# Strassen's seven products for the first 512 rows of paired weight panels

## The chip, the cores and the metric

One NeuronCore of a Trainium2 chip runs the whole program. The metric is the device time of one execution in microseconds (us). Engines are named as the profile names them: PE (TensorE) with PEld (its weight loads), DVE (VectorE), ACT (ScalarE), POOL (GpSimd), SP (SyncE, which issues most of the transfers). "L774" is line 774 of the kernel before.

## The reference, cut to what matters

Two transformer blocks run one after the other on 256 tokens of width 2048, in float32. Nearly all of the arithmetic is in products of the activations (256 x K) with large weights:

```python
proj = rmsnorm(x, g) @ w_in          # 2048 x 6144: differential attention and retention
x = x + mixed @ w_o                  # 2048 x 2048
xq = hx @ w_xq; xk = hm @ w_xk; xv = hm @ w_xv; x = x + xo @ w_xo
x = x + (silu(hf @ w_gate) * (hf @ w_up)) @ w_down      # 2048 x 5632 twice, 5632 x 2048
...
mod = silu(c) @ w_ada + b_ada        # one row times 2048 x 6144
proj = h @ w_in_2; g = sigmoid(h @ w_merge + b_merge)
merged = g_a * (y_a @ w_br_attn) + g_p * (y_p @ w_br_pool)
out = x + gate * rmsnorm(merged @ w_out)
```

## The kernel before, in words

**Panels.** `panel_table` (L152) cuts every weight into panels of 512 columns. A panel has two PSUM banks, one for each tile of 128 tokens, and sums over its rows in chunks of 512 rows. Even and odd panels use different pairs of banks (`bank_of`, L293), so one pair is emptied while the other is filled. The order is: 12 panels of `w_in` (kinds tq, v, rg), 4 each of `w_o` (o), `w_xk`, `w_xv`, `w_xq`, `w_xo`, then gate and up panels in turn (g, u), interrupted after four and eight of each by four panels of `w_down` (d, d, and e at the end), then one kv panel, 8 panels of `w_in_2` (q, ga, pu, gp), 8 of `w_merge` (m), 4 each of the two branches (ba, bp) and 4 of `w_out` (out). A panel of four chunks has 8 halves.

**Halves.** A chunk of 512 x 512 weights is one item of 1 MB, loaded by SP into one of 4 buffers (`raw`, RAWS = 4). It is used in two halves of 256 rows (128 x 1024 elements). For each half ACT rounds to `whi` (L1194) and DVE makes the rest `wlo = raw - whi` (L1762); both have 4 slots (HALVES = 4). The activations are held the same way as high and low parts, in the buffers `a` and `b`. PE then runs, for each 128 rows and each token tile, three matmuls with the activations as the stationary 128x128 operand and 512 weight columns moving (L774 to L776): high by high, high by low, low by high. A half is 2 x 2 x 3 = 12 matmuls, and there are 720 halves.

**What sets the order.** Every engine runs a program written out in full, one list of steps, one for each half. At its step n each of ACT and DVE makes the half three ahead, then one piece of a queued job (`Jobs`: attention, retention, turning of results into new stationary operands), then, at the end of a panel, takes the sum out of PSUM (`begin`). Nothing is reordered at run time: what waits holds up all that stands behind it on its engine. The waits that matter are these four. ACT makes half n only after PE has finished half n-4 (`e.wait_ge(s["half"], n - HALVES + 1)`). DVE makes the low part after ACT's high part. PE waits for the low part. SP loads item i into the buffer of item i-4 only when the low part of the last half of that item is made (`wait_taken`, L1928).

**The ada items.** `w_ada` is one row times a matrix and is done on DVE, one multiply-add over 128x2048 for each item of 1 MB (`add_ada`, L1449, L1460). 32 of these items are put between the weight items from the first up panel on, one for every two items, and 16 from the second merge panel on in the same rhythm. They use the same four buffers and the same SP queue.

Of the kernel before, what the change touches and what calls it, by code (L numbers as in the profile page):

```python
# [9 lines left out]
F32 = mybir.dt.float32  # L10
# [5 lines left out]
D = 2048  # L16
S = 256
# [51 lines left out]
def layouts(v):  # L69
# [8 lines left out]
Step = namedtuple("Step", "p half n tiles made end")  # L78
# [16 lines left out]
    "b_merge", "b_gate0", "b_gate1", "gain0", "gain1", "out",  # L95
# [5 lines left out]
    "x_hi", "x_lo", "mem_hi", "mem_lo", "st_hi",  # L101
# [50 lines left out]
def panel_table(a):  # L152
# [3 lines left out]
    def rows(version, n, first=0):  # L156
        return tuple((j * PW, (version, first + j)) for j in range(n))

    w_in, w_o, w2 = a["w_in"][0], a["w_o"][0], a["w_in_2"][0]
# [3 lines left out]
        ("tq", 4, 3072), ("tq", 5, 3584), ("v", 2, 4096), ("rg", 0, 5120), ("v", 3, 4608), ("rg", 1, 5632))]  # L163
    for kind, w, met in (("o", w_o, rows("mix", 4)), ("xk", a["w_xk"][0], mem), ("xv", a["w_xv"][0], mem),
                         ("xq", a["w_xq"][0], rows("hx", 4)), ("xo", a["w_xo"][0], rows("xo", 4))):
        table += [Panel(kind, j, w, j * PW, met, None) for j in range(4)]
    for first, n, down in ((0, 4, "d"), (4, 4, "d"), (8, 3, "e")):
        for i in range(first, first + n):
            table.append(Panel("g", i, a["w_gate"][0], i * PW, rows("hf", 4), None))
            table.append(Panel("u", i, a["w_up"][0], i * PW, rows("hf", 4), None))  # L170
        h = tuple((i * PW, ("h", i)) for i in range(first, first + n))
        done = first if down == "d" else 0
        table += [Panel(down, done + j, a["w_down"][0], j * PW, h, "last" if (down, j) == ("e", 3) else None)
                  for j in range(4)]
    table += [Panel("kv", 0, w2, 1024, mod, "first")]
    table += [Panel(kind, i, w2, col, mod, None) for kind, i, col in (
        ("q", 0, 0), ("ga", 0, 1536), ("q", 1, 512), ("ga", 1, 2048), ("pu", 0, 2560), ("gp", 0, 3584),
        ("pu", 1, 3072), ("gp", 1, 4096))]
    table += [Panel("m", 2 * n + b, a["w_merge_2"][0], b * D + n * PW, mod, None) for n in range(4) for b in range(2)]
    for n in range(4):  # L180
        table.append(Panel("ba", n, a["w_branch_attn_2"][0], n * PW, rows("ya", 2), None))
        table.append(Panel("bp", n, a["w_branch_pool_2"][0], n * PW, rows("yp", 2), None))
    table += [Panel("out", j, a["w_out_2"][0], j * PW, rows("mg", 4), "last" if j == 3 else None) for j in range(4)]
    return table
# [9 lines left out]
class Stream:  # L194
# [3 lines left out]
    def __init__(self, panels):  # L198
        self.panels, self.index = panels, {(p.kind, p.i): i for i, p in enumerate(panels)}
        self.base, n = [], 0  # L200
        for p in panels:
            self.base.append(n)
            n += 2 * len(p.rows)
        self.total = n
        self.end = self.base[1:] + [n]
        self.steps = self._steps()
        kv = self.index["kv", 0]
        self.pool_halves = range(self.base[kv], self.end[kv])
        self.items, self.item_of, self.ada_before = [], [], {}
        self._items()  # L210
        last, before, lies = {}, {}, {}
        for i, p in enumerate(panels):
            for j, (_, key) in enumerate(p.rows):
                last[key] = self.base[i] + 2 * j + 2
                at = place_of(*key)
                if lies.get(at, key) != key:
                    before[key] = lies[at]
                lies[at] = key
        self.free = {key: last[before[key]] if key in before else 0 for key in last}

    def _steps(self):
        steps, done = [], 0
        for i, p in enumerate(self.panels):
            n = 2 * len(p.rows)
            a, b = {"first": (0, HALVES), "last": (n - HALVES, n), None: (n, n)}[p.stagger]
            order = ([(h, (0, 1)) for h in range(a)] + [(h, (t,)) for t in range(2) for h in range(a, b)]
                     + [(h, (0, 1)) for h in range(b, n)])
            for h, tiles in order:
                made = min(done + HALVES, self.total)
                done += 1 in tiles  # L230
                steps.append(Step(i, h, self.base[i] + h, tiles, made, h == n - 1))
        return steps

    def _items(self):
        early = [(g, k) for g in range(2) for k in range(16)]
        late = [(2, k) for k in range(16)]
        count, ada = 0, []
        for i, p in enumerate(self.panels):
            for kc in range(len(p.rows)):
                self.ada_before[len(self.item_of)] = ada  # L240
                self.item_of += [len(self.items)] * 2
                self.items.append(("w", i, kc))
                count, ada = count + 1, []
                for todo, first in ((early, self.index["g", 0] + 1), (late, self.index["m", 1])):
                    if todo and i >= first and count % 2 == 0:
# [1744 lines left out]
```

## Time and profile before

| | |
|---|---|
| runs of the kernel before | 2140.12 us median of 3 (2139.46 to 2142.23) |
| the profiled execution's own time | 2138.73 us |
| its span | 2136.8 us |
| PE, DVE, ACT, POOL busy | 2111.2, 1258.9, 964.7, 72.1 us |
| granted PE clock, mean | 0.998 |

The span is what the trace covers; 1.9 us of the execution lie around it. A matmul's end is modelled, so its row shows 0.39 us while the next one starts 0.227 us later; the distance of starts is its cost. A busy share says how much of the time an engine had work, not whether it was waited for.

### The profile page before, as it was taken

What the parts mean: (1) busy time and instruction counts of PE and PEld (TensorE: products, weight loads), DVE (VectorE), ACT (ScalarE), POOL (GpSimd) and SP (SyncE); (2) the same over time, 40 slices, a digit from 0 to 9 for tenths busy, and PEclk for the clock granted to TensorE, in tenths of its full rate; (3) what the DMA queues carried; (4) which work ended last, traced back from release to release, by engine and by line L of the source; (5) the groups of instructions that cost most, each with busy time, mean ns of one, the idle gap of its engine ahead of it and who ended that gap; (6) DMA issues with size and microseconds to landing.
All of it is one profiled execution on the core that took longest, in us unless ns stands there. A gap on an engine that the chain in (4) does not pass through costs nothing.

```text
span 2136.8 us, 23563 instructions
## 1 busy us (share of the span) xinstructions
PE 2111.2 (99%) x9574; PEld 1743.9 (82%) x9574; DVE 1258.9 (59%) x1334; ACT 964.7 (45%) x1236; POOL 72.1 (3%) x94
## 2 busy tenths in 40 slices
PE   8999999999999999999999999999899999999998
PEld 7888888888888888888888888888688888888786
DVE  5556555644444556777677554555655545777755
ACT  6545444644443444443344433445644544444343
POOL 1000000000000000000000000000310000000000
PEclk9999999999999999999999999999999999999999
DMA  9555557555544459787887555554465556888653
GB/s 337 160 185 180 162 182 249 198 187 187 197 138 158 151 188 336 277 289 268 291 293 256 197 185 191 196 190 166 146 226 160 176 182 209 290 313 287 206 186 118
DMA packets 206284, 453.62 MB, mean 212 GB/s; under 512 B 7888, under 2 KB 10080, under 8 KB 199904
## 3 DMA queue, kind: packets, MB, share of 16 engines
q1 hardware_dynamic: 200272, 432.04, 59.1%
q0 software_dynamic: 5616, 19.94, 3.1%
q8 instruction: 76, 1.25, 0.2%
q14 instruction: 32, 0.26, 0.0%
q10 hardware_dynamic: 288, 0.13, 0.0%
HBM read 447.88 MB, written 4.19 MB: 212 GB/s over the span
## 4 chain that ended last, share of the span: by engine, by line
PE 89%; issue 6%; DVE 2%; DMA 1%; ACT 1%; POOL 0%; SPq 0%; DVEq 0%; ACTq 0%; POOLq 0%
PE ps L774 28%; PE ps L776 28%; PE ps L775 27%; PE ps L416 2%; DMA raw<-in_w_in_dram 1%; PE ps L535 1%; PE ps L556 1%; DMA FR<-in_x_t_dram 1%; PE ps L637 0%; PE ps L621 0%; DVE wlo L1762 0%; PE ps L671 0%; PE ps L660 0%; ACT FR L1057 0%; DVE FR L1583 0%
## 5 line engine op out<-in xcount | busy, mean ns | idle before, releaser
L1762 DVE TENSOR_TENSOR wlo<-raw,whi 128x1024 fp32r<-128x1024 f32 x712 | 869.0, 1224 | 648.7 <-ACT whi L1194 645.2
L1194 ACT ACTIVATE whi<-raw 128x1024 fp32r<-128x1024 f32 x720 | 758.6, 1057 | 755.4 <-PE ps L776 744.7
L774 PE MATMUL ps<-whi,ah 128*128 128x512 f32 x1888 | 751.1, 398 | 4.8 <-DVE wlo L1762 2.2
L776 PE MATMUL ps<-whi,al 128*128 128x512 f32 x1888 | 736.6, 390 | 0.0
L775 PE MATMUL ps<-wlo,ah 128*128 128x512 f32 x1888 | 735.6, 390 | 0.0
L774 PEld LDWEIGHTS ps<-whi,ah 128*128 128x128 f32 x1888 | 354.9, 188 | 77.0 <-issue 4.5
L776 PEld LDWEIGHTS ps<-whi,al 128*128 128x128 f32 x1888 | 354.6, 188 | 75.7
L775 PEld LDWEIGHTS ps<-wlo,ah 128*128 128x128 f32 x1888 | 355.2, 188 | 71.2 <-issue 0.2
L774 PE MATMUL ps<-whi,bh 128*128 128x512 f32 x992 | 392.6, 396 | 0.7 <-DVE wlo L1762 0.7
L776 PE MATMUL ps<-whi,bl 128*128 128x512 f32 x992 | 386.7, 390 | 0.0
L775 PE MATMUL ps<-wlo,bh 128*128 128x512 f32 x992 | 386.3, 389 | 0.0
L776 PEld LDWEIGHTS ps<-whi,bl 128*128 128x128 f32 x992 | 186.2, 188 | 39.6
L774 PEld LDWEIGHTS ps<-whi,bh 128*128 128x128 f32 x992 | 186.3, 188 | 39.3 <-DVE wlo L1762 1.2
L775 PEld LDWEIGHTS ps<-wlo,bh 128*128 128x128 f32 x992 | 186.4, 188 | 38.4 <-issue 1.0
L1460 DVE SCALAR_TENSOR_TENSOR FR<-raw,Z,FR 128x2048 f32<-128x2048 f32 x45 | 105.6, 2346 | 0.0
L1794 POOL TENSOR_TENSOR Z<-Z 128x2 f32<-128x2 f32 (+1 forms) x18 | 11.7, 655 | 1523.7 <-DVE Z L1237 826.9
L813 ACT ACTIVATE bh<-ps 128x512 fp32r<-128x512 f32 x38 | 22.8, 599 | 80.1 <-PE ps L416 56.6
L1247 DVE TENSOR_TENSOR bl<-ps,bh 128x512 fp32r<-128x512 f32 x38 | 26.3, 691 | 47.4 <-ACT bh L813 47.4
L416 PEld LDWEIGHTS ps<-ident,FR 128*128 128x128 f32 x312 | 38.1, 139 | 13.8 <-issue 3.5
L416 PE MATMUL ps<-ident,FR 128*128 128x128 f32 x312 | 46.1, 272 | 3.2 <-DVE FR L1276 2.2
L804 ACT ACTIVATE junk<-X 128x512 bf16<-128x512 f32 x38 | 23.9, 629 | 37.7 <-DVE X L1298 30.9
L844 ACT ACTIVATE FR<-ps,Z 128x512 f32<-128x512 f32 x22 | 15.2, 689 | 29.9 <-PE ps L776 29.9
(192 smaller groups left out, 751.2 us busy)
## 6 DMA issues: line engine op xcount, KB each, us to landing
raw<-in_w_in_dram SPq DMA_DIRECT2D x83, 1024.0 KB, 5.2
raw<-in_w_ada_dram SPq DMA_DIRECT2D x48, 1024.0 KB, 4.8
raw<-in_w_gate_dram SPq DMA_DIRECT2D x44, 1024.0 KB, 5.2
raw<-in_w_up_dram SPq DMA_DIRECT2D x44, 1024.0 KB, 5.2
raw<-in_w_down_dram SPq DMA_DIRECT2D x44, 1024.0 KB, 5.1
raw<-in_w_merge_dram SPq DMA_DIRECT2D x32, 1024.0 KB, 5.7
raw<-in_w_o_dram SPq DMA_DIRECT2D x16, 1024.0 KB, 5.1
raw<-in_w_xk_dram SPq DMA_DIRECT2D x16, 1024.0 KB, 5.0
```

The source lines that it names most:

```text
L416: ins = e.transpose(T[b].ap[:, kk * 256 + t * 128:kk * 256 + t * 128 + 128], src[:, t, (2 * b + kk) * 128:(2 * b + kk + 1) * 128], ident[: ...
L535: ins = e.matmul(A[0].ap[:, t * S:(t + 1) * S], QTC[:, d, t * 128:(t + 1) * 128], XKT[:, 4 * h + d, :], start=(d == 0), stop=(d == 3))
L556: ins = e.matmul(A[b].ap[:, dd * S:(dd + 1) * S], XV[:, k, c0:c0 + 128], PTC[:, k, :], start=(k == 0), stop=(k == 1))
L774: e.matmul(o, h, wh, start=(st.half == 0 and kk == 0), stop=False)
L775: e.matmul(o, h, wl, start=False, stop=False)
L776: ins = e.matmul(o, lo, wh, start=False, stop=(st.end and kk == 1))
L804: squares[:] = name, done(e.activation(junk[:, 0:n], in_, ACT.Square, accum_out=acc), name)
L813: ins = e.activation(hi, bank.ap[:, :], ACT.Copy)
L1194: done(e.activation(whi[:, n % HALVES, :], raw[:, i % RAWS, h * 1024:(h + 1) * 1024], ACT.Copy), "hi")
L1247: ins = e.tensor_tensor(lo, bank.ap[:, :], hi.bitcast(F32), ALU.subtract)
L1460: done(e.scalar_tensor_tensor(acc, src, csilu[:, k:k + 1], acc, ALU.mult, ALU.add), "ada")
L1762: done(e.tensor_tensor(wlo[:, n % HALVES, :], src, whi[:, n % HALVES, :].bitcast(F32), ALU.subtract), "lo")
```

## The change

**Pairs.** 80 of the 95 panels are put together in 40 pairs (f, s): all but the first two of `w_in`, the last two of the e and of the out panels, kv, and the ba and bp panels. In each pair the first 512 rows of both panels are met by Strassen's algorithm in Winograd's form. The 2 x 2 blocks are: activations, two token tiles by two halves of 256 rows; weights, two halves of rows by the two panels. Seven products of 6 matmuls take the place of 8 blocks of 6 matmuls. All other rows stay as they were. A product has one weight half and one token tile, and it counts as one entry in the whi/wlo slots, just like an ordinary half.

**Sums of weights.** Four of the seven products use a sum of weight blocks. DVE makes each with one 128x1024 tensor_tensor in place in `raw` (`sum_weights`), which waits for DVE's own last low part. The sums are spread so that each stands before a different entry's low part. The sums of activations (`make_forms`) are made once for each of 11 first chunks.

**Sums of results.** M3, M1, M2 and others add up in PSUM. ACT copies a bank in the middle of the sum three times per pair into a buffer `side` (`snapshot`), DVE makes one of them a difference, and when a panel ends, DVE adds or subtracts the side buffer for three of the pair's four banks (`summed`); residual and merge panels have it added to their other term beforehand (`add_ahead`).

**Order.** A pair of four chunks runs (N is an ordinary half of the first panel): M3, M5, N, M1, M2, N, M6, N, N, M7, N, M4, N, then six halves of the second panel. The first panel of a pair takes the banks that the pair before left earliest. No job runs at M3, M5 and M1. The ada items are placed anew: two in each of the first ten gate/up pairs (after the third and fourth chunk of u), three in each of the four d pairs and in each of the four merge pairs, one in each of the first four branch panels.

```diff
+PRODUCTS = {"M3": (0, 0, True, 1, 0), "M5": (0, 1, True, 1, 1), "M1": (1, 1, False, 0, 0),
+            "M2": (1, 0, False, 1, 0), "M6": (1, 1, True, 0, 0), "M7": (1, 1, True, 0, 1), "M4": (1, 1, False, 1, 1)}
...
+    def _pair(self, f, s):
+        i_f, i_s = self._item(f, 0), self._item(s, 0)
+        b11, b21, b12, b22 = (i_s, 0), (i_s, 1), (i_f, 0), (i_f, 1)
...
+        product("M3", b22, start=True, job=False)
+        product("M5", b12, b11, start=True, job=False)
+        normal(f, *next(todo), snap=("s5", q))
+        product("M1", b11, start=True, job=False)
+        product("M2", b21, start=True, snap=("s1", q))
+        if chunks == 4:
+            normal(f, *next(todo))
+        product("M6", b22, b12)
+        normal(f, *next(todo), snap=("v", q))
+        if chunks == 4:
+            normal(f, *next(todo))
+        product("M7", b11, b22, minus=True)
+        normal(f, *next(todo), snap=("s3", q))
+        product("M4", b21, b22, aside=q)
+        for c, hf in todo:
+            normal(f, c, hf)
+        for c in range(1, chunks):
+            for hf in range(2):
+                normal(s, c, hf)
+            if self.panels[s].kind in ("u", "d") and c > (1 if self.panels[s].kind == "u" else 0):
+                self._load_ada(self._early, 1)
+            elif self.panels[s].kind == "m":
+                self._load_ada(self._late, 1)
...
+            def snapshot(what, q):
+                form, place = {"s5": ("M5", (0, 0)), "s1": ("M1", (1, 0)), "s3": ("M7", (0, 1))}[what]
...
+                e.wait_ge(s["half"], at[form] + 1)
...
+                done(e.activation(side_of(pair[place[0]], place[1]), bank_of(pair[panel], t)[:, :], ACT.Copy), "snap")
...
+            def summed(p, t, dst):
+                wait_sum(p, t)
+                wait_side(p, t)
+                took(add_side(p, t, dst, bank_of(p, t)[:, :]), p, t)
+            def difference(q):
+                (f, second), at = stream.pairs[q]
+                e.wait_ge(s["half"], at["M6"] + 1)
...
+                done(e.tensor_tensor(v, bank_of(second, 1)[:, :], v, ALU.subtract), "snap_v")
...
+            def sum_weights(n):
+                item, h, add, minus, nth = stream.entries[n]
+                for loaded in (item, add[0]):
+                    e.wait_ge(s[f"raw{loaded % RAWS}"], 16 * (loaded // RAWS + 1))
+                if count["lo"]:
+                    e.wait_ge(s["lo"], count["lo"])
...
+                done(e.tensor_tensor(place((item, h)), place(add), place((item, h)), ALU.subtract if minus else ALU.add),
+                     "t_sum")
+            for _, at in stream.pairs:
+                sums_before |= {at["M3"]: at["M5"], at["M5"] + 1: at["M6"], at["M2"]: at["M7"], at["M6"] + 1: at["M4"]}
...
             def wait_taken(i):
...
+                    if i in stream.last_sum_of:
+                        e.wait_ge(s["t_sum"], stream.last_sum_of[i])
+                    n = stream.last_of_item[i]
                     e.wait_ge(s["lo_pool" if n in stream.pool_halves else "lo"], stream.lo_count(n))
```

## Rows read from the trace of the kernel before

**Rows 1.** The page: busy time of the engines, and shares of the last chain.

```profile
PE 2111.2 (99%) x9574; PEld 1743.9 (82%) x9574; DVE 1258.9 (59%) x1334; ACT 964.7 (45%) x1236; POOL 72.1 (3%) x94
...
PE 89%; issue 6%; DVE 2%; DMA 1%; ACT 1%; POOL 0%; SPq 0%; DVEq 0%; ACTq 0%; POOLq 0%
```

**Rows 2.** Groups of instructions: busy us, mean ns, then idle time before.

```profile
L1762 DVE TENSOR_TENSOR wlo<-raw,whi 128x1024 fp32r<-128x1024 f32 x712 | 869.0, 1224 | 648.7 <-ACT whi L1194 645.2
...
L1460 DVE SCALAR_TENSOR_TENSOR FR<-raw,Z,FR 128x2048 f32<-128x2048 f32 x45 | 105.6, 2346 | 0.0
...
L1298 DVE TENSOR_TENSOR X<-ps,X 128x512 f32<-128x512 f32 x38 | 24.5, 686 | 6.3 <-PE ps L776 6.3
...
L828 ACT ACTIVATE FR<-ps 128x512 f32<-128x512 f32 x16 | 9.6, 599 | 25.4 <-PE ps L416 25.4
```

**Rows 3.** Timeline about 1000 us: start, duration, engine, then idle before.

```profile
999.27 1.06 ACT L1194 ACTIVATE whi<-raw 128x1024 fp32r<-128x1024 f32 x1 [1.66 <-PE ps L776]
...
1000.36 1.23 DVE L1762 TENSOR_TENSOR wlo<-raw,whi 128x1024 fp32r<-128x1024 f32 x1 [1.49 <-ACT whi L1194]
...
1001.50 2.35 DVE L1460 SCALAR_TENSOR_TENSOR FR<-raw,Z,FR 128x2048 f32<-128x2048 f32 x1
...
1001.99 1.06 ACT L1194 ACTIVATE whi<-raw 128x1024 fp32r<-128x1024 f32 x1 [1.66 <-PE ps L776]
...
1003.76 1.22 DVE L1762 TENSOR_TENSOR wlo<-raw,whi 128x1024 fp32r<-128x1024 f32 x1
```

**Rows 4.** Timeline at 1010 us: the last matmul of a half, and the high part behind it.

```profile
1009.66 0.39 PE L776 MATMUL ps<-whi,bl 128*128 128x512 f32 x1
...
1010.15 1.06 ACT L1194 ACTIVATE whi<-raw 128x1024 fp32r<-128x1024 f32 x1 [1.66 <-PE ps L776]
```

**Rows 5.** Windows: length, busy PE, PEld, DVE, ACT, POOL, clock, DMA, GB/s.

```profile
483.00:527.00 44.00, 44.00 (x199) 36.43 (x198) 21.32 (x20) 18.60 (x19) 0.00 (x0) 1.00 0.58 191
...
832.00:876.00 44.00, 44.00 (x200) 36.41 (x199) 31.65 (x26) 19.21 (x20) 0.00 (x0) 1.00 0.89 319
876.00:919.00 43.00, 43.00 (x195) 35.61 (x194) 30.95 (x25) 18.04 (x19) 0.00 (x0) 1.00 0.79 279
919.00:963.00 44.00, 44.00 (x200) 36.41 (x199) 31.70 (x26) 19.10 (x20) 0.00 (x0) 1.00 0.80 283
963.00:1006.00 43.00, 43.00 (x203) 35.75 (x202) 31.70 (x31) 16.88 (x17) 0.00 (x0) 1.00 0.75 266
1006.00:1050.00 44.00, 44.00 (x195) 36.41 (x194) 31.18 (x25) 16.98 (x16) 0.00 (x0) 1.00 0.82 290
...
1789.00:1833.00 44.00, 44.00 (x197) 36.45 (x196) 30.55 (x27) 19.80 (x23) 1.08 (x2) 1.00 0.77 269
1833.00:1876.00 43.00, 43.00 (x192) 35.59 (x191) 29.80 (x25) 18.90 (x20) 1.08 (x2) 1.00 0.86 300
1876.00:1920.00 44.00, 44.00 (x196) 36.44 (x195) 31.66 (x25) 19.03 (x21) 1.08 (x2) 1.00 0.86 304
1920.00:1963.00 43.00, 43.00 (x192) 35.59 (x191) 31.34 (x27) 18.94 (x20) 1.61 (x3) 1.00 0.86 303
```

**Rows 6.** Every load into raw (its landing time), and what SP's queue waited for.

```profile
DMA to landing us min/median/max: 4.7/5.1/18.6
...
SPq L1926 <- DVE wlo L1762: 1795.6, 352, 10.7
```

**Rows 7.** Window in the burst of loads at the start.

```profile
10.00:15.00 5.00, 5.00 (x23) 3.96 (x22) 3.59 (x7) 3.99 (x8) 0.00 (x0) 1.00 1.07 376
```

**Rows 8.** Timeline of one head of the windowed attention, scores to transposes.

```profile
1625.94 1.02 PE L621 MATMUL ps<-FR 128*128 128x256 f32 x4
...
1629.94 0.66 PE L629 MATMUL ps<-ident,FR 128*128 128x128 f32 x4 [0.20 <-ACT FR L1057]
```

**Rows 9.** Windows in which PE stood longest in mid-program.

```profile
1515.00:1530.00 15.00, 11.31 (x49) 7.81 (x47) 9.96 (x21) 10.06 (x19) 11.23 (x6) 1.00 0.38 130
1530.00:1545.00 15.00, 11.40 (x53) 8.96 (x54) 8.92 (x20) 10.64 (x20) 5.47 (x5) 0.89 0.22 71
```

More of the change, by code:

```diff
@@ L172, in panel_table @@
         done = first if down == "d" else 0
[L173 to L176, printed above, removed]
+        table = [Panel(down, done + j, a["w_down"][0], j * PW, h, "last" if (down, j) == ("e", 3) else None)
+                 for j in range(4)]
+        groups += pairs(table) if down == "d" else pairs(table[:2]) + ones(table[2:])
@@ L180, in panel_table @@
     for n in range(4):
[L181 to L184, printed above, removed]
+        groups.append((Panel("ba", n, a["w_branch_attn_2"][0], n * PW, rows("ya", 2), None),))
+        groups.append((Panel("bp", n, a["w_branch_pool_2"][0], n * PW, rows("yp", 2), None),))
@@ L187, in place_of @@
+    table = [Panel("out", j, a["w_out_2"][0], j * PW, rows("mg", 4), "last" if j == 3 else None) for j in range(4)]
+    return groups + pairs(table[:2]) + ones(table[2:])
 def place_of(version, c):
@@ L194 @@
 class Stream:
[L198 to L210, printed above, removed]
-        last, before, lies = {}, {}, {}
[L212 to L232, printed above, removed]
@@ new lines, in _item, with _load_ada, _entry @@
+    def _item(self, p, c):
+        self.items.append(("w", p, c))
+        return len(self.items) - 1
+    def _load_ada(self, todo, n):
+        for _ in range(n):
+            if todo:
+                self._ada.append(len(self.items))
+                self.items.append(("ada", *todo.pop(0)))
+    def _entry(self, item, half, add=None, minus=False):
+        if add is not None:
+            self.sums += 1
+        self.entries.append(Entry(item, half, add, minus, self.sums))
+        n = len(self.entries) - 1
+        if self._ada:
+            self.ada_before[n], self._ada = self._ada, []
+        return n
@@ new lines, in _places @@
+    def _places(self):
+        last, before, lies = {}, {}, {}
+        self.last_step = {}
+        for i, st in enumerate(self.steps):
+            key = self.panels[st.p].rows[st.c][1]
+            uses = [(key, place_of(*key))]
+            if st.form and PRODUCTS[st.form][2]:
+                uses = [(form_of(key), "forms_" + place_of(*key)[0] if key[0] != "mg" else "forms_b")]
+            for what, at in uses:
+                last[what] = st.n + 1
+                self.last_step[what] = i
+                if lies.get(at, what) != what:
+                    before[what] = lies[at]
+                lies[at] = what
+        self.free = {what: last[before[what]] if what in before else 0 for what in last}
@@ L778, in tensor_program @@
+                if st.taken:
                     ins.then_inc(s["half"], 1)
```

658 lines of the change are left out of this document (505 added, 153 removed).

## The prediction

> **What bounds the kernel now.** I read the page's busy times and the shares of the last chain first. PE is busy 99% of the span and has 89% of the chain, so PE sets the time; DVE has work 59% of it [rows 1]. Next the groups by line, for the price of each kind of instruction [rows 2]. Then the timeline of a plain stretch: the high parts start at 999.27 and 1001.99, so a half of 12 matmuls takes 2.72 us, 0.227 us for each. High part (1.06), low part, and in the ada stages a 2.35 us multiply-add all fit within it [rows 3]. Then the windows by stage: where there is no ada, DVE has 21.32 us of work in 44; with ada 30 to 32 in each 43 or 44, while PE shows no gap in any of them [rows 5]. Last SP's queue: it nearly always waits for a low part, 352 times, 1795.6 us [rows 6]. So loads start when a buffer comes free, not when there is bandwidth. Today that has slack, because four buffers turn over evenly. This is what I look at below.
>
> **PE's share of the change.** Each pair replaces 48 matmuls by 42: 6 x 0.227 = 1.36 us, and 40 pairs give 54.4 us. If nothing else moved, the profiled execution would go from 2138.7 to 2084.3.
>
> **What DVE gets.** Back to back, the next instruction starts a little before the row of the last one ends: a low part costs 1001.50 - 1000.36 = 1.14 us and I take 1.13, the multiply-add 1003.76 - 1001.50 = 2.26 [rows 3]. Each pair adds three low parts (3 x 1.13 = 3.4), four sums of weights of the same shape that wait for the last low part, at 1.22 each [rows 2] (4.9), one difference out of PSUM (0.65) and for o, xo, d, e, m and the gate/up pairs three more passes of 128x512 (3 x 0.65 = 1.95; 0.69 less overlap [rows 2]); elsewhere two or three take the place of reads that DVE or ACT did, and I count 0.6. So a pair of the first sort gets 10.9 us more. ACT gets three high parts and three snapshots of 0.6 [rows 2, 3], 5 us: it has 17 to 20 in 43 [rows 5], so its throughput is safe.
>
> DVE per pair, before and after:
> - merge: 30.55 + 29.80 + 31.66 + 31.34 = 123.35 in 174 us [rows 5], 30.9 for a pair's 43.5. One ada less (-2.3), +10.9: 39.5.
> - down with ada: 31.70 + 31.18 in 87 us [rows 5], 31.4; -2.3 + 10.9: 40.0.
> - gate/up with ada: 94.3 in 131 us [rows 5], 32.0 for a pair with its turned results (44.5); two ada less (-4.5), +10.9: 38.4.
> - without ada: 21.3 in 44 [rows 5], some 31 to 32 after.
>
> All of these are below PE's 42.2 to 43.2 us. By throughput alone the change pays.
>
> **What throughput leaves out: two loads in every pair that DVE must wait for.** The first two items of a pair, i_f and i_s, hold two of the four buffers through the products. Item 4 (third chunk of f) needs i_f's buffer, free only when M4's sum has been made, before entry 7's low part. Item 5 (first chunk of s) needs i_s's, free only when M4's own low part is made. A load takes 5.1 us [rows 6], then a high part 1.06 [rows 3]: 6.2 us from release to the first low part that can use it. After the first release DVE has three low parts to do (3.4): it stands 2.8 us. After the second it has one (1.13): it stands 5.1 us, since its program is in order, though sums, side passes and ada work stand behind. Together 7.9 us per pair that DVE can't use once it is behind.
>
> Counted on an undisturbed pair: M4's high part starts when entry 7 ends on PE, 14.96 us after the pair's start; + 0.26 (PE's last matmul starts at 1009.66, its place ends 0.227 later, ACT starts at 1010.15 [rows 4]) + 1.06 + 1.22 = 17.5 release, 22.6 landed, 25.0 low part made; PE wants it at 25.84. That leaves 0.8 us, and f's third chunk already takes about 1 of them (M4's sum at 9.2, landed 14.3, low part 16.6 where PE's pace would allow 15). Pairs whose results are turned by PE meanwhile have up to 1 us more. So without ada a pair stalls little: I take 0.3 to 0.5.
>
> A loop for pairs with ada is then DVE's work + 7.9: merge 47.4, down 47.9, gate/up 46.3, against 43.5, 44.0 and 44.5 before. The first pair of each stage enters with full buffers and pays part of it, and some of the waiting falls together with PE's own pace: I take +3.3 for each of the 8 merge and down pairs (+26) and +1.0 for each of the 10 gate/up pairs (+10). Ends: the loads may hide as in today's trace (-1.36 + 0.3 each, -19 in all), or the loop holds in full and the late start spoils the next pair too (+8 for merge, where ACT's sigmoids stand between, +5 for down, +2 for gate/up: +72).
>
> The bytes are no way out: 8 loads must come after i_s is free in a merge pair (s's three, three ada, the next i_f and i_s), at 376 GB/s in a burst [rows 7] 2.8 us each, 22.4 + 2.3 for the first one's latency, 24.7 of the 24 that are left from 19.
>
> The Trainium skill (DMA: Bandwidth & Descriptors, Anatomy of one DMA) has a fixed 2.0 us plus bytes at 436 GB/s, 4.4 us for 1 MiB. The trace has 4.7 at least and 5.1 in the median [rows 6], so the row is used; by the page each of the two waits would be 0.7 us shorter and the 18 ada pairs together up to 25 us, most of the loss I find there.
>
> **Snapshots.** The N after M5 needs the snapshot at its second token tile, 1.36 us later; ACT's copy takes 0.26 + 0.6 + 0.05 = 0.9 if ACT is free [rows 2, 3]. It is not where begin() gave it work: after o, xo and m (two squares or sigmoids after DVE's two passes), 1 to 1.5 us late; after tq, xk, xq and gates about 0.3. With the 0.3 to 0.5 above this makes the 13 pairs of o, xk, xv, xq, xo, e, out and the last gate/up net -0.9 each: -12. Bounds: -1.36 and +0.5 each, -18 and +6. The snapshot is not shown for its place in the program; its price is that of the same copy out of PSUM.
>
> **Attention on short steps.** Jobs move one piece per step, and steps of 1.36 us now stand among those of 2.72. A head of the windowed attention goes from scores to transposes in 4.0 us (1625.94 to 1629.94), and PE already waits 0.20 for it with a 2.72 us step between [rows 8]. A short step takes away 1.36, and a weight sum ahead on DVE adds up to 1.2: 0.5 to 2.5 us for some of the 8 heads; the differential heads of w_in have three steps for their chain and less to lose. I take 0 net for the 5 pairs of w_in and +1 for the four q/ga and pu/gp pairs, whose 1.36 is in it: +4. Bounds: -1.36 and +3 for each of the nine, -12 and +27.
>
> The activation sums (11 times four passes, a high and a low part, some 3 us of DVE each) stand many halves ahead of their use, behind at least one whole panel: nothing, or 1 us each if late (11). Start, kv, branches and the end keep their order: 0.
>
> **Sum.** -12 + 4 + 10 + 26 = +28 on 2138.7: 2167. The median of the runs lies 1.4 above the profiled one: 2168 us (the rivals' times have the 1.4 too). All ends together, some of which exclude each other, reach from -49 (2091) to +116 (2256).
>
> **The rivals.**
> - *Supply keeps up.* The ada pairs stall like the others. For it: no gap in PE in any ada window, and DVE's sums below PE's time [rows 5]. Against: the two releases above, whose chain has no slot for another 1 us. -54.4 + 40 x 0.3 + about 5 for the heads = -37: 2103.
> - *Half of it.* The ada pairs lose just their gain and the heads nothing: -12 - 12 = -24: 2116. For it: DVE waits for the load only when it is behind, and PE's pace leaves it 3 us of slack at each entry.
> - *The late start feeds on itself* (slower). A pair that starts with DVE behind empties its last panel after two further low parts and a sum, so that the snapshot and M1 come late, M4's release too, and the next load. Place: merge, down and gate/up with ada; it decides where DVE's work + 7.9 passes PE's 43. Price +72 there instead of +36: 2204. PE's clock may add to it: after 3.7 us of standing in 15 it was granted 0.89 in the next 15 us, so it ran at 1.2 GHz for some of them [rows 9]. The Trainium skill (TensorE: Matmul & The Clock Gate, HAM oscillation) warns of just this for loads awaited tile by tile. At the row's 11% of 15 us, 1.65 us, in 18 pairs it would be 30 us.
> - *No change.* The stalls just eat 54.4.
>
> **Chances.** The forecast (2150 to 2195) 0.47, the self-feeding start (above) 0.15, small losses 0.04: slower 0.66. Supply keeps up 0.15, half 0.13: faster 0.28. Within 0.2% (4.3 us, about what a measurement of this kernel can tell) 0.06. The two signs hold most of it together, so the range runs from the better half of the first rival, 2105, to the third, 2205; the forecast's own is 2150 to 2195.
>
> **What would show it.** Right: 9574 - 240 matmuls; in merge and down windows PE gaps of 3 to 5 us per 43, ended by DVE's low part, DVE 80 to 85% busy, and DVE's idle time before low parts rooted in ACT's high part, this one waiting for a load of raw. SP's wait for DVE just before M4's release. Wrong: PE without gaps in the ada stages and a merge stage of 4 x 42; or gaps that end with the snapshot or the attention, not with low parts.

## The result, and the profile after

| | before | after |
|---|---|---|
| median of the runs (4 each) | 2140.53 us | 2289.41 us (2283.27 to 2291.96) |
| ratio | | 1.0691, 95% interval 1.0667 to 1.0714 |
| profiled execution: its span | 2136.8 us | 2289.1 us |
| granted PE clock, mean | 0.998 | 0.986 |

Slower by 149 us, where I had forecast 28. The page of the changed kernel, its busy times, the last chain and the groups that carry the change (busy us, mean ns, idle time before):

```profile
PE 2127.8 (93%) x9334; PEld 1706.2 (75%) x9334; DVE 1667.4 (73%) x1791; ACT 1166.3 (51%) x1519; POOL 72.0 (3%) x94
...
DVE 29%; PE 28%; DMA 21%; issue 12%; ACT 8%; SPq 0%; DVEq 0%; POOL 0%; ACTq 0%; POOLq 0%
...
L2226 DVE TENSOR_TENSOR wlo<-raw,whi 128x1024 fp32r<-128x1024 f32 x832 | 1000.4, 1220 | 425.9 <-ACT whi L1528 423.5
L1528 ACT ACTIVATE whi<-raw 128x1024 fp32r<-128x1024 f32 x840 | 868.4, 1054 | 699.3 <-PE ps L1019 252.7
...
L2243 DVE TENSOR_TENSOR raw<-raw 128x1024 f32<-128x1024 f32 x160 | 195.9, 1224 | 62.2 <-DVE wlo L2226 23.0
...
L1124 ACT ACTIVATE side<-ps 128x512 f32<-128x512 f32 x120 | 71.0, 592 | 44.4 <-PE ps L1019 44.1
```

The matmuls went as counted, 9574 - 240 = 9334. But PE now has gaps in 161 of 2289 us, where it had them in 26 of 2137 [rows 1], and the chain no longer runs along PE (89% before): half of it is DVE and DMA together. The other 17 us of the difference are in the busy time: 54 us less for the matmuls left out, and 71 more, of which the clock is a part. By the mean clock (1 - 0.986) x 2289 = 32 us went to the lower of its two levels (1.2 GHz), against 4 before, if PE had work all that time; the rest I can't split, since a matmul that nothing follows at once counts as busy for its modelled 0.39 us instead of 0.227.

What PE, and behind it DVE and ACT, waited for (total us, times, longest):

```profile
PE ps L1017 <- DVE wlo L2226: 63.5, 77, 3.9
PE ps L1017 <- ACT side L1124: 29.0, 13, 5.0
PE ps L1017 <- DVE side L1651: 17.6, 19, 2.0
...
DVE wlo L2226 <- ACT whi L1528: 423.5, 248, 7.0
...
ACT whi L1528 <- DMA raw<-in_w_down_dram: 77.7, 24, 5.8
ACT whi L1528 <- DMA raw<-in_w_up_dram: 70.1, 32, 4.4
ACT whi L1528 <- DMA raw<-in_w_gate_dram: 69.3, 28, 4.4
...
ACT whi L1528 <- DMA raw<-in_w_merge_dram: 55.2, 19, 5.6
ACT whi L1528 <- DMA raw<-in_w_in_dram: 42.8, 22, 4.1
...
DMA to landing us min/median/max: 4.8/7.2/16.9
```

Read upwards: loads land late, ACT's high part waits for them, DVE's low part for that, PE for the low part. The median load takes 7.2 us to land instead of 5.1 [rows 6]. Two further waits were priced far lower in the forecast: the snapshot (29.0 us, 13 times) and the passes over `side` (17.6).

One turn of a gate/up pair with ada, DVE's timeline (start, duration, what ended the idle time before), from one pair's low parts behind its first pass over `side` to the next pair's:

```profile
906.31 2.35 DVE L2226 TENSOR_TENSOR wlo<-raw,whi 128x1024 fp32r<-128x1024 f32 x2
913.86 2.36 DVE L2226 TENSOR_TENSOR wlo<-raw,whi 128x1024 fp32r<-128x1024 f32 x2 [5.20 <-ACT whi L1528]
...
929.78 1.23 DVE L2243 TENSOR_TENSOR raw<-raw 128x1024 f32<-128x1024 f32 x1 [1.56 <-DMA raw<-in_w_up_dram]
...
951.93 1.22 DVE L2226 TENSOR_TENSOR wlo<-raw,whi 128x1024 fp32r<-128x1024 f32 x1 [2.10 <-ACT whi L1528]
...
953.68 2.35 DVE L2226 TENSOR_TENSOR wlo<-raw,whi 128x1024 fp32r<-128x1024 f32 x2
```

The turn is 953.68 - 906.31 = 47.4 us where two plain panels took 44.5. DVE stands 5.20 us for the load behind M4 (5.1 forecast), 2.10 for the one behind M4's sum (2.8), and with all waits of the turn, the 0.2 ahead of weight sums too, 9.8 us; its work is the other 37.6 (38.4 forecast). Over 13 pairs in a row with ada, gate/up and down, a turn takes 48.8 us on average (47.0 to 51.2 from L1651's pass to the next pair's). The merge pairs do worse. DVE, then SP's issues, then ACT in one of them:

```profile
1962.32 1.23 DVE L2226 TENSOR_TENSOR wlo<-raw,whi 128x1024 fp32r<-128x1024 f32 x1 [2.98 <-ACT whi L1528]
...
1971.74 2.36 DVE L2226 TENSOR_TENSOR wlo<-raw,whi 128x1024 fp32r<-128x1024 f32 x2 [5.32 <-ACT whi L1528]
...
1982.15 1.23 DVE L2226 TENSOR_TENSOR wlo<-raw,whi 128x1024 fp32r<-128x1024 f32 x1 [1.65 <-ACT whi L1528]
...
1992.93 1.23 DVE L2243 TENSOR_TENSOR raw<-raw 128x1024 f32<-128x1024 f32 x1 [2.76 <-DMA raw<-in_w_merge_dram]
...
2001.90 1.23 DVE L2226 TENSOR_TENSOR wlo<-raw,whi 128x1024 fp32r<-128x1024 f32 x1 [1.64 <-ACT whi L1528]
```

```profile
1955.88 9.85 SPq L2425 DMA_DIRECT2D raw<-in_w_merge_dram  x2
1965.78 0.50 SPq L2425 DMA_DIRECT2D raw<-in_w_ada_dram  x1
1966.32 0.42 SPq L2425 DMA_DIRECT2D raw<-in_w_merge_dram  x1
1966.79 0.80 SPq L2425 DMA_DIRECT2D raw<-in_w_ada_dram  x1
```

```profile
1970.64 2.01 ACT L1528 ACTIVATE whi<-raw 128x1024 fp32r<-128x1024 f32 x2 [4.08 <-DMA raw<-in_w_merge_dram]
1976.83 1.06 ACT L1528 ACTIVATE whi<-raw 128x1024 fp32r<-128x1024 f32 x1 [4.18 <-DMA raw<-in_w_merge_dram]
1979.94 1.23 ACT L1398 ACTIVATE FR<-FR 128x512 f32<-128x512 f32 x2 [2.04 <-DVE FR L2058]
1981.07 1.05 ACT L1528 ACTIVATE whi<-raw 128x1024 fp32r<-128x1024 f32 x1
```

Five waits, 14.4 us. The two that I had forecast are there at their size (2.98 + 5.32 = 8.3 us, forecast 7.9); three are new. The 2.76 us are a wait for a load that landed 7.2 us after its issue. The 1.65 and the 1.64 aren't waits for a load: before both of these low parts ACT stood for DVE (2.04 us the first time), did two sigmoids and only then the high part, which DVE had to wait for. The late release of one buffer holds the whole queue of loads: the second merge load goes out late, at about 1965.4, and the next three within 1.5 us behind it, because other buffers had come free meanwhile. ACT has the first at 1970.64 and the merge load issued at 1966.32 only at 1976.83, 10.5 us later. Such a burst isn't special to merge: in the gate/up turn above four loads go out between 907.60 and 909.10 and land after 5.1, 7.4, 9.4 and 11.5 us. In windows of about one pair each (length, busy PE, PEld, DVE, ACT, POOL, clock, DMA, GB/s) the first is gate/up, the others are merge:

```profile
893.00:940.00 47.00, 44.12 (x194) 34.97 (x193) 39.20 (x39) 24.63 (x29) 0.00 (x0) 1.00 0.62 224
...
1903.00:1956.00 53.00, 45.84 (x195) 36.48 (x194) 37.73 (x38) 23.68 (x29) 1.08 (x2) 0.97 0.58 208
1956.00:2010.00 54.00, 45.00 (x183) 34.48 (x182) 38.75 (x35) 22.79 (x26) 1.07 (x2) 0.97 0.63 224
```

Against [rows 5] the DMA engines are *less* busy in merge (0.58 and 0.63, before 0.77 to 0.86) and DVE has 72%: neither is full. From one pass of L1651 to the next the merge turns take 56.5, 54.0 and 53.4 us. These and the 47.4 are the turn of a loop, not a throughput.

### The profile page after: what moved, and what is told of

Same layout as the page of the kernel before. It is cut to its first block, busy times and chain, and to the rows that moved or that the text cites. A ratio compares the mean times of both kernels' runs of the same rounds, so it can differ in the third digit from the quotient of the medians.

```text
span 2289.1 us, 24836 instructions
## 1 busy us (share of the span) xinstructions
PE 2127.8 (93%) x9334; PEld 1706.2 (75%) x9334; DVE 1667.4 (73%) x1791; ACT 1166.3 (51%) x1519; POOL 72.0 (3%) x94
## 4 chain that ended last, share of the span: by engine, by line
DVE 29%; PE 28%; DMA 21%; issue 12%; ACT 8%; SPq 0%; DVEq 0%; POOL 0%; ACTq 0%; POOLq 0%
DVE wlo L2226 14%; PE ps L1017 8%; PE ps L1019 8%; PE ps L1018 8%; DMA raw<-in_w_up_dram 6%; ACT whi L1528 5%; DVE raw L2243 4%; DMA raw<-in_w_merge_dram 3%; DMA raw<-in_w_down_dram 3%; DMA raw<-in_w_in_dram 2%; DVE FR L1893 2%; DMA raw<-in_w_gate_dram 2%; DMA raw<-in_w_o_dram 1%; PE ps L609 1%; DVE FR L1629 1%
## 5 line engine op out<-in xcount | busy, mean ns | idle before, releaser
L2226 DVE TENSOR_TENSOR wlo<-raw,whi 128x1024 fp32r<-128x1024 f32 x832 | 1000.4, 1220 | 425.9 <-ACT whi L1528 423.5
L1528 ACT ACTIVATE whi<-raw 128x1024 fp32r<-128x1024 f32 x840 | 868.4, 1054 | 699.3 <-PE ps L1019 252.7
L1017 PE MATMUL ps<-whi,ah 128*128 128x512 f32 x1618 | 654.5, 405 | 46.7 <-DVE wlo L2226 26.8
L1019 PE MATMUL ps<-whi,al 128*128 128x512 f32 x1618 | 634.6, 392 | 0.0
L1018 PE MATMUL ps<-wlo,ah 128*128 128x512 f32 x1618 | 634.2, 392 | 0.0
L2243 DVE TENSOR_TENSOR raw<-raw 128x1024 f32<-128x1024 f32 x160 | 195.9, 1224 | 62.2 <-DVE wlo L2226 23.0
L1017 PE MATMUL ps<-whi,fah 128*128 128x512 f32 x208 | 87.9, 423 | 29.2 <-DVE wlo L2226 16.9
L1124 ACT ACTIVATE side<-ps 128x512 f32<-128x512 f32 x120 | 71.0, 592 | 44.4 <-PE ps L1019 44.1
L1018 PE MATMUL ps<-wlo,fah 128*128 128x512 f32 x208 | 83.1, 400 | 0.0
L1019 PE MATMUL ps<-whi,fal 128*128 128x512 f32 x208 | 83.0, 399 | 0.0
L1017 PEld LDWEIGHTS ps<-whi,fah 128*128 128x128 f32 x208 | 40.1, 193 | 46.8 <-DVE wlo L2226 37.9
```

What stands on the lines that cost most here:

```text
L1017: e.matmul(o, xh[:, k, tokens], wh, start=first, stop=False, skip_group_check=more)
L1018: e.matmul(o, xh[:, k, tokens], wl, start=False, stop=False, skip_group_check=more)
L1019: ins = e.matmul(o, xl[:, k, tokens], wh, start=False, skip_group_check=more, stop=kk == 1 and (st.end or st.form in READ))
L1124: done(e.activation(side_of(pair[place[0]], place[1]), bank_of(pair[panel], t)[:, :], ACT.Copy), "snap")
L1528: done(e.activation(whi[:, n % HALVES, :], raw[:, item % RAWS, h * 1024:(h + 1) * 1024], ACT.Copy), "hi")
L2226: done(e.tensor_tensor(wlo[:, n % HALVES, :], src, whi[:, n % HALVES, :].bitcast(F32), ALU.subtract), "lo")
```

## The experiments

The loads divide the run into stages. Times in us between the first loads issued for each matrix (e.g. "xk" from the first of `w_xk` to the first of `w_xv`; "gu" from the first gate load to the first down load, "ffn" from there to the last down load, "in2" to the first merge load):

```
        w_in      o    xk    xv    xq    xo    gu   ffn    in2     m    br   out
before 274.8   94.0  91.6  88.9 104.2 105.7 188.6 546.2  246.9 190.9  81.5 123.5
after  288.7  101.7 106.2  89.1 105.4 116.3 208.4 592.0  256.7 226.6  75.4 122.6
e1     283.2   97.5 103.2  86.4 102.5 112.1 189.0 545.7  250.1 217.2  75.4 122.4
e2     282.4  101.3 104.4  87.8 103.2 111.2 196.7 560.6  248.8 218.0  75.3 122.2
e3     282.5   98.3 106.7  87.8 103.4 112.0 204.0 581.9  254.0 224.5  75.4 122.3
e4     275.6   93.9  92.2  89.0 105.1 105.6 190.7 545.4  246.3 193.2  79.2 124.4
e5     287.4   98.7 102.2  86.5 103.2 112.3 194.9 561.6  255.6 211.8  75.4 122.6
e6     273.9   91.7  95.6  86.3 100.1 106.4 184.9 533.3  241.6 205.2  75.4 122.3
e7     288.9   97.0 102.1  86.5 103.4 110.8 189.0 543.7  255.5 192.9  79.3 122.1
e8     277.3   93.9  92.0  88.1 102.9 112.1 188.9 543.5  247.3 193.2  79.2 123.5
e9     286.5   92.1  91.3  89.0 104.6 107.6 191.6 541.3  255.7 215.6  75.4 123.5
e10    283.5   89.6  91.5  89.0 106.2 106.0 186.8 529.9  261.5 200.0  74.3 131.1
e11    288.5   92.6  95.5  86.5 103.2 108.0 197.0 556.9  254.6 199.0  76.5 122.2
e12    271.7   94.1  91.5  89.0 100.7 109.1 186.8 529.9  249.4 198.4  74.0 130.9
e13    271.2   94.0  91.6  89.0 100.6 109.2 190.7 540.3  250.2 198.4  74.1 131.1
e14    275.7   93.9  92.0  89.0 104.2 105.6 193.2 537.9  246.3 193.2  79.2 123.5
```

In the expectations theory A is the late load: two buffers are held through the products, the loads behind them start late, and DVE, in program order, stands for them. Its rivals put the loss on what was added to DVE, or on the snapshots. The table is of the profiled executions; that of e5 ran 10 us above the median of its four runs. A border is the issue of a load and can move by itself: with five buffers (e10, e12, e13) it comes some 4 us earlier against e4, so that w_in is shorter and out 7 longer, and runs with merge pairs and four buffers have 3 to 4 us less in "br" than e4. So I compare five buffers with five. In e1, e2, e3 and e6 what is left out changes the output; the other kernels compute all of the reference.

### e1: two loads less

```diff
-                items[p, c] = self._item(p, c)
+                reused = chunks == 4 and (p, c) in ((f, 3), (s, 1))
+                items[p, c] = items[f, 2] if reused else self._item(p, c)
```

Two chunks of a pair are not loaded; their halves are taken from another chunk's buffer.

> The changed kernel (2289 us), but in each pair of four chunks the third chunk of the first panel and the first ordinary chunk of the second panel are not loaded; their halves are taken from the buffer of the first panel's second chunk (the output is then another one). So no load of the pair stands right behind the release of the two pinned buffers, and 78 MB less are loaded; DVE, ACT and PE have the same instructions. Theory A (DVE and ACT stand in their order waiting for these two loads, 7.9 us a pair where DVE is behind): 18 pairs with ada lose some 6 us each and the other 21 pairs 1 to 2 us, so 2130 to 2170 us. Theory B (DVE's own added work, 10.9 us a pair, sets the time): within 30 us of the changed kernel, 2260 to 2290. Theory C (the snapshots that PE waits for): the same as B.

2184.05 us, ratio 1.0201 (1.0180 to 1.0222): 105 us come back without an instruction less on DVE, short of theory A's 2130 to 2170 and far from B's 2260. The same views as above:

```profile
PE ps L1018 <- ACT side L1125: 29.0, 13, 5.0
PE ps L1018 <- DVE wlo L2227: 23.8, 27, 3.1
...
DMA to landing us min/median/max: 4.7/5.2/16.4
```

Gate/up and down are back at 189.0 and 545.7, as before the change. The waits for low parts fall from 63.5 to 23.8 and the median landing to 5.2; the snapshot's 29.0 stay to the tenth: another cause. Merge stays at 217.2. This run also loads 78 MB less, and so doesn't separate the late start from the bytes; e5 does.

### e2: small sums of weights

```diff
-done(e.tensor_tensor(place((item, h)), place(add), place((item, h)), ...
+done(e.tensor_tensor(place((item, h))[:, 0:8], place(add)[:, 0:8], place((item, h))[:, 0:8], ...
```

The weight sums are made over 8 columns only; waits and order stay.

> The changed kernel, but each of the 160 sums of weights covers 8 columns instead of 1024 (other output): every wait stays, DVE has 160 x 1.1 = 176 us less to do. Theory A: the loop of a pair with ada is DVE's work + the loads waited for, so 4.4 us less in each of the 18 pairs with ada, and a little in the others because the releases come 1 us earlier: -90 to -120, 2170 to 2200. Theory B: nearly the whole of it, -150 or more, below 2140. Theory C: -20 at most.

2212.67 us, ratio 1.0335 (1.0314 to 1.0355): 77 us, from 1667.4 - 1509.1 = 158 us less work on DVE. So DVE's work counts too, at half its size; theory A had 2170 to 2200.

### e3: no snapshots

The three copies to `side`, the difference and the waits for them are left out; `side` is zero.

> The changed kernel without the 120 snapshots on ACT and the 40 differences on DVE, and without PE's waits for them; the side buffer is set to zero once and is still added (other output). PE's records show 29.0 us waited for the snapshots and 17.6 for the difference. Theory A: the difference stands behind a load, so most of its 17.6 us come back as a wait for the next low part; the 29 after o, xo and merge panels are half kept: -20 to -40, 2250 to 2270. Theory C: at least the 46.6 us that are waited for, and what the late start costs behind, -60 or more, below 2230.

2256.30 us, ratio 1.0539 (1.0517 to 1.0560): 33 us. The waits that named the snapshot are gone and a part has become waits for low parts:

```profile
PE ps L1011 <- DVE wlo L2214: 88.6, 91, 3.6
```

A wait's 29.0 + 17.6 us in the table of waits is thus not what its removal brings back.

### e4: no pairs

All else of the changed kernel (ada placement, banks, forms), but each panel by itself.

> The changed kernel's program with no panel paired: all rows of all panels as ordinary halves, no sums of weights, snapshots or side buffer; the sums of activations, the copies for them, the jobs' order and the new places of the ada items stay. If pairing is the whole cause: 2135 to 2150 us, as the kernel before. If the new places of the ada items or the activation sums cost something by themselves, it is above 2150.

2143.42 us, ratio 1.0013 (1.0004 to 1.0023). The new placement costs 3 us; all of the rest is the pairs.

### e5: M4 one ordinary half earlier

```diff
-        if chunks == 4:
-            normal(f, *next(todo))
         product("M7", b11, b22, minus=True)
         normal(f, *next(todo), snap=("s3", q))
         product("M4", b21, b22, aside=q)
```

The ordinary half comes after M4 instead, and the difference stands ahead of DVE's low part of its step.

> The changed kernel in another order, nothing left out: in pairs of four chunks M3, M5, N, M1, M2, N, M6, N, M7, N, M4, N, N instead of M6, N, N, M7, N, M4, N; the difference on DVE stands before the low part instead of behind it. M4 releases the second pinned buffer one ordinary half earlier and the load behind it has one ordinary half more before it is needed; the third chunk of the first panel is needed one product later. Theory A (loads behind the two releases): about 2.7 us a pair in the pairs that wait for it, 18 to 35 pairs: -50 to -90, so 2200 to 2240. Theory B (DVE's work): the same work in the same time, 2280 to 2300.

2204.42 us, ratio 1.0314 (1.0292 to 1.0337): 85 us from order alone, the same instructions. The second of the held buffers comes free one ordinary half (2.72 us) earlier; the first one's release, M4's sum, keeps its place, but its load is needed one product later. What the place of the difference adds was not run by itself. It is four fifths of what e1 gave, with all bytes loaded, in the same stages (gate/up and down -44, merge -15). The median landing is still 6.9 us: when a load starts, and what stands behind it, counts more here than how long it takes.

### e6: e1, e2 and e3 together

> The changes of the runs with two loads less, small sums and no snapshots in one kernel (other output). PE keeps its 9334 matmuls. Alone they gave -105, -77 and -33. If these three are the whole cost of the pairs, 2085 to 2110: the gain of 54 us from the matmuls is there. Theory A (the waits share a loop, one removed makes room for the others): the sum -215 can't be reached and it stops near PE's bound, 2090 to 2105. If it stays above 2125, something else (attention on short steps, the clock, more products per slot) has a share.

2118.94 us, ratio 0.9905 (0.9886 to 0.9925). Alone the three gave 105, 77 and 33, 215 in all, together 170: they are links of one loop, and each shortens it. That is above the 2085 to 2110 that I expected if they were the whole cost. Only now do the seven products show a gain, 25 us below e4 of the 54. Merge still has +12 on e4 and xk +3.

### e7: pairs only outside the ada stages

The order of e5, 22 pairs (none in merge, down and the ten gate/up pairs with ada).

> The order with M4 earlier, and pairs only where no ada item is among their loads: w_in, w_o, w_xk, w_xv, w_xq, w_xo, the last gate/up pair, e, w_in_2, out (22 of 40 pairs); the others as ordinary halves. Nothing is left out. PE saves 22 x 1.36 = 30 us. Before the merge these stages took in the changed kernel some 56 us more than in the kernel before (w_in 14, w_o 8, w_xk 15, w_xo 11, w_in_2 10). Theory A: the new order takes away most of the loads' part but not the snapshots' and the attention's: 2130 to 2150. Theory B: 2150 to 2180.

2171.99 us, ratio 1.0147 (1.0127 to 1.0167). In theory B's range, not A's. The ada stages are at e4's times to within 2 us. The 22 pairs that I had put at -8 us cost +29 against e4: w_in +13, o +3, xk +10, xo +5, in2 +9; xv, xq and out gain 2 each. e5 to e7, the 18 ada pairs, is 32 us.

### e8: seven pairs

The order of e5; pairs in xv, xq, xo and the last gate/up.

> The same order with pairs only of w_xv, w_xq, w_xo and the last gate and up panels (7 pairs), where DVE has least to do and PE's turning of results gives room. Nothing is left out. PE saves 9.5 us. Theory A: most of it is kept, 2132 to 2140, faster than the kernel before by 0.1 to 0.4%. Theory B and C: the waits eat it, 2140 to 2150.

2144.03 us, ratio 1.0019 (1.0010 to 1.0029), level with e4, as B and C had it. xv and xq gain 0.9 and 2.2, of 2.7 each that the matmuls are worth; xo loses 6.5.

### e9 and e10: four and five raw buffers

26 pairs (five of w_in, xq, all gate/up, in2, merge: those whose activations lie in buffer `a`), in e5's order; the sums of `b` are not kept, and their room holds a fifth buffer in e10 (`RAWS = 5`).

> The order with M4 earlier, pairs only of w_in, w_xq, gate/up, w_in_2 and merge (26 pairs); w_o, w_xk, w_xv, w_xo, down, e and out as ordinary halves, so only one set of activation sums is needed (8 KB per partition come free and stay unused). Nothing is left out. It is the base of the next run. From the stages of the run with M4 earlier (w_in +13, w_xq -1, gate/up +5 for the first four and about 12 more, w_in_2 +9, merge +20): 2190 to 2205.

> The run before with five buffers for weights of 1 MB instead of four (the 8 KB that came free) and nothing else. The third chunk of the first panel no longer waits for the first pinned buffer, and the first chunk of the second panel follows M4's sum instead of M4's low part. Theory A (loads started late because two buffers are pinned): both waits nearly vanish, 26 pairs x 2 to 3 us: 2120 to 2150. Theory B (DVE's added work and the snapshots): at most 10 us less than with four.

2173.57 (1.0151, 1.0131 to 1.0171) and 2150.95 us (1.0048, 1.0031 to 1.0065): the fifth buffer gives 23 us, theory A, if a little short of its 2120 to 2150; e9 had been expected at 2190 to 2205. Gate/up and ffn fall to 186.8 + 529.9 = 716.7 against 734.8 before, merge from 215.6 to 200.0. ACT's waits for loads, with four and with five:

```profile
ACT whi L1545 <- DMA raw<-in_w_up_dram: 55.0, 29, 3.3
ACT whi L1545 <- DMA raw<-in_w_gate_dram: 49.3, 27, 4.9
ACT whi L1545 <- DMA raw<-in_w_merge_dram: 36.7, 16, 4.9
```

```profile
ACT whi L1545 <- DMA raw<-in_w_in_dram: 10.2, 7, 3.5
ACT whi L1545 <- DMA raw<-in_w_merge_dram: 8.2, 6, 2.8
```

The waits for up and gate loads are gone. In merge and br together the pairs cost 19 us with four buffers (e9 against e4) and 2 with five (e10 against e13 below, which has no pairs). In all e10 is still 9 us above e13: gate/up and ffn gain 14, w_in loses 12, in2 11 and xq 6. What e10 keeps is thus mostly w_in and in2, and PE's waits have other names:

```profile
PE ps L1030 <- ACT side L1141: 16.6, 10, 3.1
PE ps L848 <- ACT FR L1389: 7.6, 8, 1.6
PE ps L1030 <- DVE wlo L2264: 4.5, 5, 1.4
```

### e11: squares and sigmoids behind the snapshots

The order of e5; ACT's squares of a finished residual panel and the merge sigmoids are put off by two steps, so that M5's snapshot doesn't stand behind them.

> The run with M4 earlier (2204 us), but ACT's squares after w_o and w_xo panels and its sigmoids after merge panels are done two steps later, behind the first snapshot of the next pair, instead of ahead of it. Nothing is left out. If the snapshots are late because of this work (2 to 5 us each at 8 to 12 places; PE's records show 27.0 us waited for snapshots in that run): -15 to -30, 2175 to 2190. If the snapshots are only waited for because everything is late: within 5 us of 2204.

2184.78 us, ratio 1.0209 (1.0193 to 1.0226): 20 us less than e5. o -6.1, xk -6.7, xo -4.3, merge -12.8, the stages that had this work; ffn -4.7. All these are by the table, whose e5 is 10 us high; in all they make 32 us of spans where the medians give 20. PE's wait for the snapshot, in e5 and then here:

```profile
PE ps L1015 <- ACT side L1122: 27.0, 14, 3.5
```

```profile
PE ps L1015 <- ACT side L1122: 8.9, 7, 3.0
```

### e12, e13, e14: gate/up alone

e12 has the eleven gate/up pairs and no others, e5's order and five buffers. e13 is the same without pairs, e14 the same as e12 with four buffers.

> The changed kernel with pairs in gate and up alone (those beside ada included), the order of e5 and five raw buffers in place of four. Theory A (a pinned raw buffer starts the next loads late, a fifth buffer gives a pair of this stage its loads in time): the gate/up stages keep what e10 had (186.8 and the following 530, against 188.6 and 546 before), the pairs of w_in and down no longer cost anything: 2118 to 2132 us, ratio 0.990 to 0.996. Theory B (the gain of e10 in gate/up is only five buffers helping the plain order, the pairs add nothing): the same as the run without pairs and five buffers, 2135 to 2150.

> No pairs at all and five raw buffers: the control of e12. Theory A: the plain order hardly waits for loads, so a fifth buffer gives it nothing: 2136 to 2146 us. Theory B: what e10 gained in gate/up is seen here too: 2120 to 2132.

> As e12 with four raw buffers. Theory A: the pairs of gate/up hold two buffers longer and their next loads start late, which takes back what TensorE saves: 2143 to 2160 us. Theory B: the count of buffers does not matter to the pairs: within 5 us of e12.

e12 2127.34 us, ratio 0.9942 (0.9930 to 0.9955); e13 2142.38, 1.0011 (1.0002 to 1.0019); e14 2136.84, 0.9986 (0.9977 to 0.9995). e12 is faster than both kernels, by 13 us (0.6%, clear of the interval) than the one before. Against e13 it gains 15.0 us, and eleven pairs of six matmuls are 11 x 1.36 = 15.0: with the load in time a pair of this stage gives all it promises, and the fifth buffer by itself gives nothing. The same stretch in e12 and in e14 (windows, columns as above), and in each DVE's wait at the low parts behind M4. In e12 what ACT waited for there was PE, not a load; over the run ACT waited 1.7 us for gate and up loads in e12 and 90.5 in e14:

```profile
890.00:934.00 44.00, 44.00 (x200) 36.42 (x199) 38.32 (x37) 24.05 (x27) 0.00 (x0) 1.00 0.67 240
```

```profile
939.21 1.06 ACT L1545 ACTIVATE whi<-raw 128x1024 fp32r<-128x1024 f32 x1 [1.23 <-PE ps L1032]
940.30 2.59 DVE L2264 TENSOR_TENSOR wlo<-raw,whi 128x1024 fp32r<-128x1024 f32 x2 [1.07 <-ACT whi L1545]
```

```profile
890.00:934.00 44.00, 43.20 (x193) 34.99 (x193) 37.20 (x35) 23.62 (x26) 0.00 (x0) 1.00 0.65 239
```

```profile
946.29 2.36 DVE L2264 TENSOR_TENSOR wlo<-raw,whi 128x1024 fp32r<-128x1024 f32 x2 [2.92 <-ACT whi L1545]
```

With five buffers DVE does 38.32 us of work in 44 and PE has no gap. e14 missed theory A's range (2143 to 2160) on the good side: 6.6 us of the gain are kept against e4, 5.5 against e13. That DVE catches up in the plain down panels between the pairs would explain it, but no run shows it.

## Why the prediction was wrong

**Right:** the direction; the matmuls' worth (6 x 0.227 us, shown by e12 against e13); DVE's work per pair (37.6 against 38.4); and the mechanism. Two loads per pair start late, DVE stands for them in order, and it is a loop of work plus waits with neither DVE nor the DMA engines full (e1, e5, e10).

**The step that failed, by its size:** "I take +3.3 for each of the 8 merge and down pairs (+26) and +1.0 for each of the 10 gate/up pairs (+10)". Measured: gate/up and ffn +65.6 and merge +35.7, together +101 where my terms give +34 (with the last gate/up and the e pair at -0.9). Two things in it were wrong.
- *The discount.* My own loops were 46.3 us for gate/up and 47.9 for down, 46.8 over both; the trace shows 48.8, +4.4 a pair. I had cut them to +1.0 and +3.3 because the first pair of a stage enters with full buffers and "some of the waiting falls together with PE's own pace". Neither shows: no turn of the 13 is under 47.0, and the first takes 51.1. Undiscounted my loops come to +49 for the 18 pairs, so the larger part of the shortfall is the next point.
- *The waits counted.* My two waits per pair are there and of the right size (8.3 us in the merge turn, 7.3 in the gate/up turn, forecast 7.9). I had no others; the merge turn has three more, 6.1 us, and takes 53.4 to 56.5 us instead of 47.4. One of them (2.76 us, and 1.56 in gate/up) is for a load that lands late because others were issued just before it (10.5 us for one of them, median 7.2 for all). I had that number, 2.8 us for each further MiB [rows 7], and used it only for the bytes of a pair, not to lengthen single loads. The other two (3.3 us) are the chain from DVE's pass over ACT's sigmoids to the high part, which I had only in the words "where ACT's sigmoids stand between". e11, which moves the sigmoids, takes 12.8 us out of merge by the table, but it frees the snapshot and this chain at once and doesn't separate them. Each pair so begins behind. This is the rival *The late start feeds on itself*, in which I had +8 for merge (measured +8.9, or 7.4 with "br", whose border moved), +5 for down and +2 for gate/up (measured 4.4 over both); with +72 in all it was nearest, still some 30 short, and it had 0.15.

**The second step:** "net -0.9 each: -12" for the 13 pairs without ada, and 0 and +1 for those with attention. Measured: o to xo +34, w_in +14, in2 +10, together +58 instead of -5. e7 has this by itself (+29 with M4 earlier). I had the snapshot "1 to 1.5 us late" behind squares and sigmoids; at the first pair of xk it is this (ACT's timeline, then PE's):

```profile
424.16 0.63 ACT L1048 ACTIVATE junk<-X 128x512 bf16<-128x512 f32 x1 [4.54 <-DVE X L1728]
...
425.54 1.99 ACT L1528 ACTIVATE whi<-raw 128x1024 fp32r<-128x1024 f32 x2
427.43 0.58 ACT L1124 ACTIVATE side<-ps 128x512 f32<-128x512 f32 x1
```

```profile
428.06 0.80 PE L1017 MATMUL ps<-whi,bh 128*128 128x512 f32 x1 [5.00 <-ACT side L1124]
```

ACT stood 4.54 us for DVE's residual passes, which were themselves behind, and then the squares and two high parts came before the copy: PE stood 5.00 us. I had priced the work ahead of the snapshot, not the wait of that work. e11 takes 17 us out of o, xk and xo by the table.

**Attention on short steps:** PE's wait at the heads of the second block grew from 2.3 us in all, one of them the 0.20 in [rows 8], to 4.9 in the changed kernel and 7.6 in e10. That is in the bounds, but w_in +12 and in2 +12 in e10 against e12 are more than those heads and the snapshots of these stages show. In e6 both stages are below e4. By the table no single cause has them: the two loads, the small sums and the missing snapshots (e1, e2, e3) take 5.5, 6.3 and 6.2 us out of w_in and 6.6, 7.9 and 2.7 out of in2, all three together (e6) 15 out of each. Why a fifth buffer takes nothing out of them stays open.

**The clock:** 28 us more than before by its mean. It fell to 1.2 GHz in nearly all stages: the mean is 0.98 over gate/up (807 to 1016), 0.98 over merge (1865 to 2091) and 0.95 in xk (390 to 497). I had it in the rival only, at 30 us for the 18 ada pairs. That the number comes out is luck: of sixteen falls before the end of the program seven lie in or at the edge of those stages, about 12 of the 32 us.

**The sum** on stages: forecast -5 + 34 - 1 (the out pair) = +28, measured +58 + 101 - 7 (branches and end) = +152, the difference of the spans.

## What to carry over

A transformation that saves matmuls pays only if the inputs that it holds longer don't delay the next loads: count for each buffer when it is released, when the next load lands, and what of the same program stands behind the first instruction that needs it. If a loop through "release, load, use, release" comes out longer than the compute, take it whole for every turn, and add the queueing of loads that one late release lets out together. Put such products first where one more buffer gives them their loads in time, and check each stage by itself: eleven pairs in gate/up with five buffers gained 13 us, 26 pairs in five kinds of stage with five buffers still lost 10, and forty with four lost 149.

## What the runs showed that I had not expected

- A load of 1 MB lands after 4.8 us at least in the changed kernel, but of four issued within 1.5 us in the merge pair above, the third took 10.5 us; it landed 11.5 us after the first was issued. The Trainium skill (DMA: Bandwidth & Descriptors, Anatomy of one DMA) has 2.0 us plus bytes at 436 GB/s, given for loads that GpSimd issues, where these are issued by SP. Applied to the queue, 2.0 us and three times 2.4, it makes an estimate of 9.2 us for the third, 2.2 us short of the trace.
- A change of order alone, M7 and M4 one ordinary half earlier and the difference ahead of one low part, with no instruction less, was worth 85 us of 2289.
- The share of gaps in a pair didn't tell where the clock fell. It did so within or right behind single stops of PE of 2.0 to 5.0 us: at 884.24 in gate/up, where PE had stood 2.25 us until 884.14 (0.76 from 882 to 889), while the gate/up window above, whose stops are 1.35 us at most, has 1.00. Not every such stop did it (2.55 us until 1080.13, and no fall). The Trainium skill (TensorE: Matmul & The Clock Gate, HAM oscillation) warns of waits for loads in such loops, with a fall in every turn; here it was seven falls at most in 18 pairs. All falls cost some 28 us by the mean clock, the gaps themselves 136.
